# Heads in pairs on the array's halves, the attention steps at the front of each iteration, and remainders written over the raw weights

## What is computed

```python
x = layernorm(DN_ALPHA_2 * x + 0.5 * swiglu(x, ffn_w13[i, 0], ffn_w2[i, 0]), ln_g[i, 0], ln_b[i, 0])
y = hybrid_mixer(x, w_in[i], conv_w[i], a_log[i], dt_bias[i], dn_norm_g[i], sinks[i],
                 w_branch_a[i], w_branch_b[i], w_out[i], pos_bias)
x = layernorm(DN_ALPHA_2 * x + y, ln_g[i, 1], ln_b[i, 1])
x = layernorm(DN_ALPHA_2 * x + 0.5 * swiglu(x, ffn_w13[i, 1], ffn_w2[i, 1]), ln_g[i, 2], ln_b[i, 2])
```

```python
s = jnp.einsum('bqkgd,bskd->bkgqs', qi, ki) + bias
valid = in_band & ((i > 0) | key_in_own_block)
s = jnp.where(valid, s, NEG_INF)
m = jnp.maximum(s.max(-1, keepdims=True), sk)
p = jnp.exp(s - m)
p = p / (p.sum(-1, keepdims=True) + jnp.exp(sk - m))
return jnp.einsum('bkgqs,bskd->bqkgd', p, vi)
```

## Time and profile before

| | us |
|---|---|
| median of 3 runs | 2248.57 |
| lowest and highest | 2247.88, 2250.63 |
| the profiled execution's own time | 2250.65 |
| its span in the profile | 2248.8 |
| busy: TensorE, VectorE, ScalarE, GpSimd | 2156.7, 1666.3, 1125.9, 350.3 |
| loop of the first mixer and what surrounds it, 1000 to 1141 us: TensorE, VectorE, ScalarE | 139.66, 126.63, 99.10 of 141.00 |

### The profile page before, as it was taken

One profiled execution on the slowest core, in us unless ns is written; L12 is line 12 of the kernel. 1 busy time (PEld: TensorE's weight loads), 2 busy tenths in 40 slices (PEclk: granted clock), 3 DMA queues, 4 the chain that ended last, 5 costly groups with the idle time before them and its releaser, 6 DMA issues.

```text
span 2248.8 us, 33574 instructions
## 1 busy us (share of the span) xinstructions
PE 2156.7 (96%) x13896; PEld 1927.9 (86%) x13896; DVE 1666.3 (74%) x2043; ACT 1125.9 (50%) x1486; POOL 350.3 (16%) x306
## 2 busy tenths in 40 slices
PE   4889999998999999999999999999999999999998
PEld 4768898987888888899889988888889988998887
DVE  6878898698776766669866686677666996767666
ACT  3344444797434444456664454454445767445442
POOL 2111324321120210030021140012003001212000
PEclk9899999999999999999999999999999999999999
DMA  9749894443465465755532455546576554335562
GB/s 358 241 140 339 288 327 160 120 118 113 157 207 187 157 213 184 176 180 154 130 114 76 149 170 206 187 151 224 188 188 167 154 139 113 94 114 181 193 205 94
DMA packets 304971, 396.78 MB, mean 176 GB/s; under 512 B 48031, under 2 KB 263705, under 8 KB 304820
## 3 DMA queue, kind: packets, MB, share of 16 engines
q1 hardware_dynamic: 285440, 336.75, 47.0%
q0 software_dynamic: 18496, 57.59, 8.1%
q10 hardware_dynamic: 884, 0.30, 0.1%
HBM read 393.53 MB, written 1.07 MB: 175 GB/s over the span
## 4 chain that ended last, share of the span: by engine, by line
PE 72%; DVE 17%; ACT 5%; issue 3%; DMA 1%; POOL 0%; SPq 0%; DVEq 0%; ACTq 0%; POOLq 0%
PE tiles L551 14%; PE tiles L524 8%; PE tiles L525 8%; PE tiles L526 8%; PE tiles L553 7%; PE y_rows L524 6%; PE y_rows L525 6%; PE y_rows L526 6%; DVE weights_lo L1467 4%; PE tiles L955 2%; DVE ada_acc L1515 2%; ACT weights_hi L1073 2%; DMA ada_ring<-in_ada_w_dram 1%; DVE rnn_gates L1815 1%; ACT xt L1110 1%
## 5 line engine op out<-in xcount | busy, mean ns | idle before, releaser
L1467 DVE TENSOR_TENSOR weights_lo<-weights_raw,weights_hi 128x2048 fp32r<-128x2048 f32 (+2 forms) x316 | 766.1, 2436 | 338.3 <-ACT weights_hi L1073 337.9
L1073 ACT ACTIVATE weights_hi<-weights_raw 128x2048 fp32r<-128x2048 f32 (+2 forms) x316 | 591.5, 1878 | 153.5 <-PE y_rows L526 100.7
L524 PE MATMUL tiles<-xt_hi_lo,weights_hi 128*128 128x256 f32 (+1 forms) x1824 | 522.4, 286 | 16.5 <-ACT xt L1110 7.0
L525 PE MATMUL tiles<-xt_hi_lo,weights_hi 128*128 128x256 f32 (+1 forms) x1824 | 516.6, 283 | 0.0
L526 PE MATMUL tiles<-xt_hi_lo,weights_lo 128*128 128x256 f32 (+1 forms) x1824 | 516.5, 283 | 0.0
L524 PEld LDWEIGHTS tiles<-xt_hi_lo,weights_hi 128*128 128x128 f32 (+1 forms) x1824 | 343.3, 188 | 30.5 <-issue 24.5
L525 PEld LDWEIGHTS tiles<-xt_hi_lo,weights_hi 128*128 128x128 f32 (+1 forms) x1824 | 343.6, 188 | 1.0
L526 PEld LDWEIGHTS tiles<-xt_hi_lo,weights_lo 128*128 128x128 f32 (+1 forms) x1824 | 343.5, 188 | 0.0
L551 PE MATMUL tiles<-xt_hi_lo,weights_hi 128*128 128x512 f32 x1376 | 343.4, 391 | 0.0
L551 PEld LDWEIGHTS tiles<-xt_hi_lo,weights_hi 128*128 128x128 f32 x1376 | 250.3, 189 | 46.7
L524 PE MATMUL y_rows<-weights_hi,hid_hi 128*128 128x512 f32 x608 | 239.4, 394 | 1.1 <-DVE weights_lo L1467 1.1
(11 more groups left out here) (376 smaller groups left out, 3134.6 us busy)
## 6 DMA issues: line engine op xcount, KB each, us to landing
weights_raw<-in_ffn_w_dram SPq DMA_DIRECT2D x132, 1024.0 KB, 5.1
weights_raw<-in_mlp_w_dram SPq DMA_DIRECT2D x64, 1024.0 KB, 6.6
weights_raw<-in_w_in_dram SPq DMA_DIRECT2D x52, 1024.0 KB, 5.4
ada_ring<-in_ada_w_dram POOLq DMA_DIRECT2D x76, 512.0 KB, 5.3
weights_raw<-in_rnn_w_in_dram SPq DMA_DIRECT2D x16, 768.0 KB, 4.7
weights_raw<-in_w_in_dram SPq DMA_DIRECT2D x32, 256.0 KB, 4.6
weights_raw<-in_w_branch_a_dram SPq DMA_DIRECT2D x32, 256.0 KB, 4.8
weights_raw<-in_w_branch_b_dram SPq DMA_DIRECT2D x8, 1024.0 KB, 5.1
```

The costliest lines, as they stand in the source:

```text
L524: pe.matmul(o, a, c, start=first, stop=False)
L525: pe.matmul(o, a, d, start=False, stop=False)
L1073: act.activation(slot_view(WHI, m, NSPL), slot_view(RAW, m, NRAW), ACT.Copy).then_inc(*inc("hi_ready", m))
L1467: dve.tensor_tensor(slot_view(WLO, m, NSPL), slot_view(RAW, m, NRAW), slot_view(WHI, m, NSPL).bitcast(F32), ALU.subtract).then_inc(*inc("l ...
```

## The change

**Weight ring.** `NRAW` is 5 and `NSPL` is 4. `WLO` lies over `RAW`: the remainder of slot n is written where its raw weights were. A raw buffer is therefore free only when TensorE has ended its slot, and `load(n)` waits for `slot_end[n-5]` in place of `lo_ready` of n-3. Rounding and remainder go three slots ahead, not two. Only three slots are asked for at the start (`N_RAW_FIRST`), since the first rows of the modulation weights lie over the other two; slot 3 waits until they are used.

**Pairs.** `scores` becomes `score_pair`: in every even iteration both heads' first products, then both heads' second ones, on alternating halves of the array's rows. `mix` becomes `mix_pair`, one iteration later, with 256 columns in the first product in place of twice 128. `probs_a_t` has three buffers.

**Order.** On ScalarE the exponentials of head j-1 stand at the front of iteration j, ahead of the rounding and of the slot's copy. On VectorE `norm_a(j-1)` stands at the front of iteration j, ahead of SiLU, remainder, convolution and scores.

Two semaphores get the names of others. The bias rows move to another place in SBUF.

```diff
-NRAW = 3
-NSPL = 3
+NRAW = 5
+NSPL = 4
+N_RAW_FIRST = 3
...
         RAW = put("weights_raw", [P, NRAW, SLOT])
+        WLO = put("weights_lo", [P, NRAW, SLOT], F32R, at=base)
         WHI = put("weights_hi", [P, NSPL, SLOT], F32R)
-        WLO = put("weights_lo", [P, NSPL, SLOT], F32R)
...
             def load(n):
+                if n == N_RAW_FIRST:
+                    sp.wait_ge(*past("ada_used", N_FIRST - 1))
                 if n >= NRAW:
-                    sp.wait_ge(*past("lo_ready", n - NRAW))
+                    sp.wait_ge(*past(*slot_end[n - NRAW]))
...
-                def scores(j):
-                    t, hh = divmod(j, 2)
-                    lo, hi = 64 * hh, 64 * hh + 64
-                    if j == 0:
+                def score_pair(t):
+                    if t == 0:
                         pe.wait_ge(*past("free_A", (s, "ka", 0)))
-                    bank = topen((s, "sc", j), "D")
-                    pe.matmul(bank[:, 0:P], QA[lo:hi, t, 0:P], KA[lo:hi, t // 4, 0:P], start=True, stop=True)
-                    pe.matmul(bank[:, P:384], QA[lo:hi, t, P:S], KA[lo:hi, t // 4, :], start=True, stop=True).then_inc(*inc("tile_done", (s, "sc", j)))
+                    bank = [topen((s, "sc", 2 * t + hh), "D") for hh in range(2)]
+                    part = [slice(64 * hh, 64 * hh + 64) for hh in range(2)]
+                    for hh in range(2):
+                        pe.matmul(bank[hh][:, 0:P], QA[part[hh], t, 0:P], KA[part[hh], t // 4, 0:P], start=True, stop=True)
+                    for hh in range(2):
+                        pe.matmul(bank[hh][:, P:384], QA[part[hh], t, P:S], KA[part[hh], t // 4, :], start=True, stop=True).then_inc(*inc("tile_done", (s, "sc", 2 * t + hh)))
...
+                def mix_pair(t):
+                    pe.wait_ge(*past("free_A", (s, "pt", 2 * t + 1)))
+                    pe.wait_ge(*past(*(("free_D", (s, "oa", t - 2)) if t >= 2 else ("y_free", (s - 1, 1)))))
+                    bank = y_bank(2 + t % 2)
+                    o = [bank[64 * hh:64 * hh + 64, :] for hh in range(2)]
+                    v = [VA[:, :, (2 * (t // 4) + hh) * 64:(2 * (t // 4) + hh + 1) * 64] for hh in range(2)]
+                    pt = [PTA[:, (2 * t + hh) % 3, :] for hh in range(2)]
+                    for hh in range(2):
+                        pe.matmul(o[hh][:, 0:S], v[hh][:, 0, :], pt[hh][:, 0:S], start=True, stop=True)
+                    for hh in range(2):
+                        ins = pe.matmul(o[hh][:, P:S], v[hh][:, 1, :], pt[hh][:, 2 * P:3 * P], start=False, stop=True, skip_group_check=True)
+                    ins.then_inc(*inc("tile_done", (s, "oa", t)))
...
-                    if j < 16:
-                        scores(j)
+                    if j < 16 and j % 2 == 0:
+                        score_pair(j // 2)
                     if 2 <= j < 18:
                         turn(j - 2)
-                    if j >= 3:
-                        mix(j - 3)
+                    if j >= 4 and j % 2 == 0:
+                        mix_pair(j // 2 - 2)
...
                 for j in range(19):
+                    if 1 <= j <= 16:
+                        norm_a(j - 1)
                     if 2 <= j < 18:
                         silu(j - 2)
...
-                    if 1 <= j <= 16:
-                        norm_a(j - 1)
```

61 lines of the change are left out of this document (23 added, 38 removed).

## The result

| | before | changed |
|---|---|---|
| median of the runs, us | 2248.23 | 2287.12 |
| lowest and highest, us | 2247.78, 2250.63 | 2285.93, 2287.28 |
| profiled execution, us (span) | 2250.65 (2248.8) | 2285.93 (2284.1) |

The changed kernel takes 1.0168 of the time before, 95% interval 1.0155 to 1.018: 39 us more. The forecast was 2288. One execution of the kernel before and one of a later kernel (e5) took 5.7 and 5.8 ms and are left out of all comparisons.

The account below looks back on a forecast made before the run. It took a closed chain of ScalarE and VectorE as the changed loop's bound. 36.0 + 4.4 + 1 - 2 = +39.4 on 2250.65 gave 2290, so 2288 us for the median, which lies 2.1 lower; range 2274 to 2302.

Parts of the forecast that it names:

- closed chain: Attention loop, from one negated maximum to the next: exponentials, rounding, remainder, convolution, scores, two hand-overs; 9.39 us a turn.
- TensorE sets the pace: Kernel before, attention loop: TensorE has 8.08 us of work in an iteration of 8.08 us, VectorE 7.87.
- faster rival: Attention loop turns in less than TensorE's pair, so the halves pay: 2222 to 2246, about 2235 us; chance 0.08.
- (1): Attention loop, T(0) to T(11) (T(j): VectorE has written head j's negated maximum): 9.39 us a turn, +18.0 us a block.
- (2): Four iterations with z slots, T(11) to T(15): exponentials now behind the squares; +2.2 us a block, bounds 0 and +4.
- (3): Loop end, behind T(15): last two value products go together; +0.5 us a block, +1 in all, bounds 0 and +3.
- (4): Head pairs on the array's halves: worth 0 on the path; 1.64 us saved a pair if they overlap fully.
- (5): Weight ring: TensorE's wait for remainders, 3.4 us, can be won; late landings may cost; -2 us, bounds -4 and +6.
- (6): Pauses lower the clock, inside the loop shortening only the next wait; 0 us, bounds 0 and +5.
- The signs: Changed kernel's profile: T(j) 9.4 us apart, VectorE idle 1.3 and 0.3 us, TensorE waiting 2.6 to 4.3 us at scores.

Follow-up runs that it names:

- e5: The changed kernel with only VectorE's normalising put back to the end of the iteration: 2287.75 us, ratio 1.0167.
- e1: The changed kernel with ScalarE's exponentials and VectorE's normalising back at the end of the iteration; pairs and new ring stay: 2250.93 us, ratio 1.0003.
- e2: e1 with one head's scores and products at a time again, so old order, single heads and new ring: 2245.33 us, ratio 0.998.
- e4: The changed kernel with ScalarE's rounding of the next weight slot put ahead of the exponentials: 2282.9 us, ratio 1.0146.
- e7: The changed kernel with the edits of e4 and e5 together: 2244.68 us, ratio 0.9983.
- e3: The changed kernel with one head's scores and products at a time again; new order and ring stay: 2286.9 us, ratio 1.0165.

## Why the prediction was right, point by point

**What bounds the kernel.** The closed chain bounds the changed kernel, as forecast. "TensorE sets the pace", said of the kernel before, doesn't hold for the convolution iterations. There the maxima are 7.72 and 8.05 us apart, which is VectorE's bare work, and T(0) to T(11) doesn't change when TensorE's iteration falls from 8.07 to 7.25 us (e1 against e2). VectorE reads the scores of head 4 5.5 us after their first product starts and those of head 11 only 4.4 us after, so it is behind TensorE and catches up. The forecast took T(0) to T(11) before from the trace and so wasn't hurt by this, and e1 shows that VectorE would have held back the pairs' saving in these iterations, on which the faster rival rests, without the closed chain too.

**(1) Convolution iterations.** Forecast 9.39 us a turn and +18.0 a block; measured 9.40 and +18.1. The links were shown one by one: without the rounding in the chain 9.05 (e4, forecast 9.06), without the normalising still 9.40 (e5), with both opened 7.7 and 8.05 (e7).

**(2) z iterations.** Forecast +2.2 a block, measured +2.0, but not spread as forecast: T(11) to T(13) +0.6 instead of +1.1, T(13) to T(15) +1.4 instead of +1.1. The stretch from the exponentials of head 11 to those of head 12, sized at 8.0 us, takes 7.4 (1105.90 to 1113.34). The +1.1 from T(13) to T(15) came near by luck. It was the price of the exponentials of head 14 behind the squares; but those of head 13, as long, no longer stand between the decay row and the squares. What is new in it is the table load of 1.28 us ahead of the exponentials (1136.01). In the kernel before the second load came behind the rounding, outside the chain:

```profile
1122.72 1.89 ACT L1073 ACTIVATE weights_hi<-weights_raw 128x2048 fp32r<-128x2048 f32 x1
...
1125.11 1.28 ACT L1323 ACT_TABLE_LOAD   x1
```

**(3) Loop end.** Forecast +0.5 a block; the change as a whole gives -1.3 and +0.7 there, the order alone (e3 against e2) 0.0 and +1.4. The rest is the ring's and the scatter of single executions, which these runs don't separate.

**(4) Pairs.** Worth nothing on the path of the changed kernel, as forecast (e3: 0.2 us). The upper bound of what they save was the true one: 0.85 us for two heads' scores. The 0.1 us for a change of shape shows too: in the kernel before the first scores product starts 0.21 us behind the slot's last (1061.91 to 1062.12), where the slot's products are 0.12 us apart. By the rule cited from the Trainium skill (TensorEngine Tiling (Array Packing), Key Properties) different tiles work in parallel; the trace agrees. What I missed is that a pair also changes which tile each slot gets. That is 5.6 us with the old order (e1 against e2), and hidden in the new one.

**(5) Ring.** Forecast -2, bounds -4 and +6; measured some -4.5 (e2), with an interval of -2.5 to -6.7: larger than forecast, and at the edge of its bounds. What was sized too low is TensorE's wait for remainders. I took 3.4 us in 7 places and left out a second row of the same view of the kernel before, the same wait in front of the products into y_rows:

```profile
PE y_rows L524 <- DVE weights_lo L1467: 1.1, 2, 0.6
```

And such a wait costs more than its length. TensorE's timeline of the kernel before, behind 0.55 us of it:

```profile
270.21 0.47 PE L524 MATMUL y_rows<-weights_hi,hid_hi 128*128 128x512 f32 x1 [0.55 <-DVE weights_lo L1467]
...
271.48 0.63 PE L525 MATMUL y_rows<-weights_lo,hid_hi 128*128 128x512 f32 x1
...
274.62 0.40 PE L524 MATMUL y_rows<-weights_hi,hid_hi 128*128 128x512 f32 x1
274.86 0.40 PE L525 MATMUL y_rows<-weights_lo,hid_hi 128*128 128x512 f32 x1
```

Eight matmuls start 0.35 to 0.43 us apart, later ones 0.24: with the slower ones ahead, 1.5 us more. The granted clock is 0.50 from 272 to 274. In e2, where the same matmuls follow without a wait, they start 0.23 us apart from the third on and the clock is 1.00. Late landings, the other bound, didn't show.

**(6) Clock.** The pauses lowered it, but not each one. In the first block it stood at 0.50 for some 3 to 7 us behind each of the six waits at the scores, of 1.75 to 4.21 us. In the second it did so for some 3 us behind those of 4.57, 4.58 and 5.59 us, and not behind those of 1.85, 2.82 and 3.05:

```profile
1844.88 0.49 PE L873 MATMUL tiles<-ka_t,qa_t 64*128 64x128 f32 x4 [3.05 <-DVE probs_a L1907]
```

From 1844.88 to 1848.88 the clock is 1.00. T(0) to T(11) is 103.45 us in both blocks, so as forecast a lower clock only used up the next wait.

**The signs.** Maxima 9.4 apart; VectorE idle for 1.24 and 0.25 us, released as written; ScalarE released by the maximum; both loops 20.2 us longer. TensorE's waits at the scores were expected at 2.6 to 4.3 us; there are six a block of 1.75 to 5.59 us, together 15.9 us in the first block and 22.5 in the second, where the clock is lower for less of the time. The sum came out 4 us high against the spans (39.4 against 35.3), 2.5 of it in term (5) and 1.6 in term (3). Against the medians, which are 38.9 apart, it is within 1 us. That closeness is partly luck: the two terms are off by more, and single executions of one kernel differ by up to 3 us. What the runs bear out is the 36 us of term (1).

## What to carry to other kernels

Before an instruction is moved to the front of an iteration, follow who is queued behind it on its engine, and whether that work leads back to the event it waits for. Here two such paths closed at once; opening one gave 4 us or nothing, opening both 42. Where buffers are handed out by order of opening, pairing two users moves every later user to another buffer, so look up who frees that one. And a saving on the busiest engine is worth nothing until the engine beside it has room: the same pairs cost 5.6 us, gave nothing, or gave 12.3 us.
